# Hybrid conformer and S5 block on 8 cores: the scan's transposes moved from TensorE to DMA, weight casts moved to other stages

## What is computed

```python
h = concat([meta, x])                       # 16 meta tokens + 2048 tokens, width 2048
xn = rmsnorm(h, norm_g)
v_c, g_c, z_c, u_s, z_s, gl_c, gl_s = split(xn @ w_in)      # 5 x 1024 and 2 x 2048 columns
y_c = silu(layernorm(causal_conv31(v_c * sigmoid(g_c)))) * silu(z_c)
y_s = gelu(s5_scan(u_s))                    # 64 groups of 16 channels, 64 complex states each
y_s = y_s * sigmoid(y_s @ w_glu + b_glu) * silu(z_s)
merged = sigmoid(gl_c + b) * (y_c @ w_conv) + sigmoid(gl_s + b) * (y_s @ w_ssm)
out = rmsnorm(h + merged @ w_out, final_g)[meta dropped]
```

## Time and profile before

| | |
|---|---|
| median of 3 runs | 1659.02 us (1658.43 to 1659.34) |
| the profiled execution | 1657.35 us, span of its slowest core 1655.8 us |
| TensorE (PE) busy | 1606.9 us, 97% of the span, mean granted clock 0.99 |
| VectorE (DVE) busy | 746.7 us, 45% |
| ScalarE (ACT) busy | 508.0 us, 31% |
| GpSimd (POOL) busy | 142.5 us, 9% |
| chain that ended last | PE 91%, ACT 3%, DMA 2%, issue 2%, DVE 1% |

### The profile page before, as it was taken

The page is one execution under the profiler, slowest core; times in us unless marked ns, Lnnn a source line. Parts: engine busy times, 40 slices in busy tenths (PEclk is TensorE's granted clock), DMA queues, the critical chain, the costliest instruction groups (busy, mean ns, idle before and its releaser), DMA issues.

```text
span 1655.8 us, 23121 instructions; the slowest of 8 cores (1653.8 to 1655.8 us)
## 1 busy us (share of the span) xinstructions
PE 1606.9 (97%) x8885; PEld 785.3 (47%) x9054; DVE 746.7 (45%) x1126; ACT 508.0 (31%) x741; POOL 142.5 (9%) x228
## 2 busy tenths in 40 slices
PE   5899999999999999999999999999999999999998
PEld 2444555555554444455444444444444444444444
DVE  3673799888840003567625211111111347443333
ACT  4763577777742110003312332111111000021112
POOL 1001333333310000000000000000000000000000
PEclk8999999999999999999999999999999999999999
DMA  9823255999449210024342524022221536455553
GB/s 223 219 87 52 49 118 93 138 136 152 96 92 176 43 19 6 12 36 61 65 57 39 89 52 64 1 38 39 39 38 39 165 115 209 148 172 152 153 153 121
DMA packets 60926, 155.43 MB, mean 94 GB/s; under 512 B 31425, under 2 KB 34625, under 8 KB 51649
## 3 DMA queue, kind: packets, MB, share of 16 engines
q0 software_dynamic: 13456, 58.20, 23.9%
q1 hardware_dynamic: 19906, 88.91, 17.3%
q10 hardware_dynamic: 27456, 6.82, 2.4%
HBM read 178.03 MB, written 40.89 MB: 132 GB/s over the span
## 4 chain that ended last, share of the span: by engine, by line
PE 91%; ACT 3%; DMA 2%; issue 2%; DVE 1%; POOL 0%; ACTq 0%; DVEq 0%; SPq 0%; POOLq 0%
PE ps L257 89%; DMA wu<-wu 2%; PE ps L276 2%; ACT cs L229 1%; DMA xt<-x 1%; ACT L229 1%; DVE xs L245 0%; ACT xs L231 0%; ACT gst L229 0%; ACT tt L229 0%; PE ps L260 0%; ACT jk L231 0%; DVE h L245 0%; DVE pt L235 0%; POOL wu L279 0%
## 5 line engine op out<-in xcount | busy, mean ns | idle before, releaser
L257 PE MATMUL ps<-xm,wr 128*128 128x512 bf16 x1238 | 288.7, 379 | 4.2 <-ACT gst L229 1.9
L257 PE MATMUL ps<-wb,xm 128*128 128x512 bf16 x1000 | 221.6, 381 | 1.7 <-issue 0.6
L257 PE MATMUL ps<-xm,zr 128*128 128x512 bf16 x1000 | 220.6, 379 | 1.3
L257 PE MATMUL ps<-wo,m 128*128 128x512 bf16 (+1 forms) x1019 | 220.1, 376 | 1.1
L257 PEld LDWEIGHTS ps<-xm,wr 128*128 128x128 bf16 x1280 | 119.3, 98 | 128.1 <-issue 5.2
L257 PE MATMUL ps<-xm,gr 128*128 128x512 bf16 x752 | 168.7, 379 | 0.8
L257 PEld LDWEIGHTS ps<-wo,m 128*128 128x128 bf16 x1040 | 101.8, 98 | 119.5
L257 PEld LDWEIGHTS ps<-wb,xm 128*128 128x128 bf16 x1024 | 100.0, 98 | 120.2 <-issue 2.4
L257 PEld LDWEIGHTS ps<-xm,zr 128*128 128x128 bf16 x1024 | 99.9, 98 | 119.2
L231 ACT ACTIVATE jk<-h 128x2048 bf16<-128x2048 f32 (+2 forms) x20 | 31.4, 1569 | 324.3 <-DVE h L245 324.3
L257 PE MATMUL ps<-wu,xm 128*128 128x512 bf16 x496 | 116.4, 389 | 13.9 <-DMA wu<-wu 7.8
(11 more groups left out here) (179 smaller groups left out, 1763.6 us busy)
## 6 DMA issues: line engine op xcount, KB each, us to landing
xt<-x SPq DMA_DIRECT2D x16, 1024.0 KB, 9.1
x<-x SPq DMA_DIRECT2D x16, 1024.0 KB, 8.8
out<-h SPq DMA_DIRECT2D x15, 1024.0 KB, 6.1
wr<-wm POOLq DMA_DIRECT2D x20, 512.0 KB, 11.6
gscr<-gst SPq DMA_DIRECT2D x20, 512.0 KB, 11.8
gr<-gscr SPq DMA_DIRECT2D x20, 512.0 KB, 4.4
wob<-wo POOLq DMA_DIRECT2D x8, 1024.0 KB, 27.7
zr<-wm POOLq DMA_DIRECT2D x16, 512.0 KB, 6.9
```

Source lines behind the costliest of these rows:

```text
L257: return S.op("pe", lambda e: e.matmul(out_, lhsT, rhs, start=start, stop=stop), r, w, signal=signal)
```

## The change

Three things. `ugt(q + 1)` of the loop becomes `ug_dma(q + 1)`: one `dma_start_transpose` on ScalarE's queue, at the end of step 1 and no longer in step 2, and the meta column's copy moves with it; only `ugt(0)` ahead of the loop stays. `btr` becomes one `dma_start_transpose` on ScalarE's queue, at its place. `ug` rows grow from 129 to 144 columns, so that the transposed part starts at a multiple of 32 bytes, and neighbouring tiles are shifted. Third, the casts leave the scan loop: the 20 small ones go to the second half of the gate g projection (8) and to the first v projection (12), the 8 large ones to the first merges, two in each of j = 0 to 3. The diff, without the changed offsets:

```diff
-        UG = [T(f"ug{i}", [128, 4, 2, 129], BF16, UGo[i]) for i in range(2)]
+        UGs = [dsrc() for _ in range(2)]
+        UG = [T(f"ug{i}", [128, 4, 2, 144], BF16, UGo[i]) for i in range(2)]
...
+        def ug_meta(q):
+            s = q % 2
+            uv = UG[s].ap.rearrange("p g r c -> p (g r) c")
+            cp("dve", uv[:, :, 15:16], UGM.ap[:, 4 * q:4 * q + 4, :].rearrange("p g r -> p (g r)").unsqueeze(2),
+               r=(UGMb,), a=(UGb[s],))
...
+        def ug_dma(q):
+            s = q % 2
+            S.op("act", lambda e: e.dma_start_transpose(
+                out=UG[s].ap.rearrange("p g r c -> p (g r) c")[:, :, 16:144],
+                in_=U.ap[:, 4 * q:4 * q + 4].rearrange("p g r t h -> p (g r t h)")),
+                 (UB[q],), (), (UGb[s],), src=UGs[s])
+            ug_meta(q)
...
         def btr(b, par):
             ys = b % 2
-            bk = misc()
-            pT = ps[bk].bitcast(BF16)
-            for t in range(8):
-                tr(pT[:, t * 128:(t + 1) * 128], YST[ys].ap[:, par, t, :], ident, r=(YSTb[ys][par], IDPb),
-                   w=(PB[bk],), signal=(t == 7))
-            cp("dve" if par == 0 else "act", YS.ap[:, b, par * 1024:(par + 1) * 1024], pT, r=(PB[bk],),
-               w=(YSB[b][2 * par], YSB[b][2 * par + 1]))
+            S.op("act", lambda e: e.dma_start_transpose(
+                out=YS.ap[:, b, par * 1024:(par + 1) * 1024].rearrange("p (t c) -> p t c", t=8),
+                in_=YST[ys].ap[:, par].rearrange("p t c -> p (t c)")),
+                 (YSTb[ys][par],), (YSB[b][2 * par], YSB[b][2 * par + 1]), src=YSs[ys][par])
...
-        casts = [("w", 0, i) for i in range(10)] + [("o", n, h) for n in range(4) for h in range(2)]
-        casts += [("w", 1, i) for i in range(10)]
+        casts = [("w", p, i) for p in range(2) for i in range(10)] + [("o", n, h) for n in range(4) for h in range(2)]
...
                     prep_g2(q)
+                    if nx:
+                        ug_dma(q + 1)
                 if st == 2 and nx:
-                    ugt(q + 1)
                     prep_g1(q + 1)
                     prep_g2a(q + 1)
-                if st % 2 == 0:
-                    cast((S.eng["pe"]["src"], S.eng["pe"]["src"].count))
...
                 tok_unit(WB[nb], WBb[nb], j, bk)
+                if nb == 1 and j % 2 == 1:
+                    cast((S.eng["pe"]["src"], S.eng["pe"]["src"].count))
...
             tok_unit(WB[2 + nb], WBb[2 + nb], j, bk)
+            if nb == 0 and j < 12:
+                cast((S.eng["pe"]["src"], S.eng["pe"]["src"].count))
...
                 stt(M0.ap[:, j, n * 512:(n + 1) * 512], MA[2 * tn + 1].ap, 0.5, MA[2 * tn].ap, ALU.mult, ALU.add,
                     r=(MAb[2 * tn], MAb[2 * tn + 1]), w=(M0B[j][n],))
+                if n % 2 == 1:
+                    cast((S.eng["pe"]["src"], S.eng["pe"]["src"].count))
```

More of the change, by code:

```diff
@@ L612, in build @@
         SSb = [t.buf() for t in SS]
-        UGo = (D0 + 90592, D0 + 49344)
-        UG = [T(f"ug{i}", [128, 4, 2, 129], BF16, UGo[i]) for i in range(2)]
+        UGo = (D0 + 90752, D0 + 49344)
+        UGs = [dsrc() for _ in range(2)]
+        UG = [T(f"ug{i}", [128, 4, 2, 144], BF16, UGo[i]) for i in range(2)]
         UGb = [t.buf() for t in UG]
-        CQo = (D0 + 75840, D0 + 51424)
+        CQo = (D0 + 76032, D0 + 51648)
         WT, G1, G2, WV, TT, CM, M7 = [], [], [], [], [], [], []
@@ L627, in build @@
         WTb, G1b, G2b, WVb, TTb, CMb, M7b = [[t.buf() for t in L_] for L_ in (WT, G1, G2, WV, TT, CM, M7)]
-        CSo = (D0 + 82304, D0 + 57312)
+        CSo = (D0 + 82496, D0 + 57536)
         CS = [T(f"cs{i}", [128, 4, 2, NCH], F32, CSo[i]) for i in range(2)]
         CSb = [t.buf() for t in CS]
-        BCT = [T(f"bct{i}", [128, 4, 4, 16], F32, D0 + 92704 + 1024 * i) for i in range(4)]
+        BCT = [T(f"bct{i}", [128, 4, 4, 16], F32, D0 + 93056 + 1024 * i) for i in range(4)]
         BCTb = [t.buf() for t in BCT]
         BCTs = [dsrc() for _ in range(4)]
-        MT = [T(f"mt{i}", [128, 4, 8, 16], F32, D0 + 67648 + 2048 * i) for i in range(4)]
+        MT = [T(f"mt{i}", [128, 4, 8, 16], F32, D0 + 67840 + 2048 * i) for i in range(4)]
         MTb = [t.buf() for t in MT]
-        DM7 = [T(f"dm7{i}", [128, 4, 16], F32, D0 + 81728 + 256 * i) for i in range(2)]
+        DM7 = [T(f"dm7{i}", [128, 4, 16], F32, D0 + 81920 + 256 * i) for i in range(2)]
         DM7b = [t.buf() for t in DM7]
@@ L744, in prep_t @@
                 r=(PB[bk],), w=(TTb[s],))
-        MP = T("mp", [128, 4, 8, 16], F32, D0 + 65600)
+        MP = T("mp", [128, 4, 8, 16], F32, D0 + 65792)
         MPb = [MP.buf(0, 1024), MP.buf(1024, 2048)]
-        MQ = [T("mq0", [128, 2, 8, 16], F32, D0 + 96800), T("mq1", [128, 2, 8, 16], F32, LWOFF + 8224)]
+        MQ = [T("mq0", [128, 2, 8, 16], F32, D0 + 97152), T("mq1", [128, 2, 8, 16], F32, LWOFF + 8224)]
         MQb = [t.buf() for t in MQ]
@@ L795, in ugt @@
             uv = UG[s].ap.rearrange("p g r c -> p (g r) c")
-            cp("dve", uv[:, :, 1:129], pT.rearrange("p (i c) -> p i c", i=8), r=(PB[bk],), a=(UGb[s],))
-            cp("dve", uv[:, :, 0:1], UGM.ap[:, 4 * q:4 * q + 4, :].rearrange("p g r -> p (g r)").unsqueeze(2),
-               r=(UGMb,), a=(UGb[s],))
+            cp("dve", uv[:, :, 16:144], pT.rearrange("p (i c) -> p i c", i=8), r=(PB[bk],), a=(UGb[s],))
+            ug_meta(q)
[5 more added lines that the diff above has]
+                 (UB[q],), (), (UGb[s],), src=UGs[s])
+            ug_meta(q)
         def vmm(g):
             s, gi, v = (g // 4) % 2, g % 4, g % 2
-            rhs = UG[s].ap[:, gi].rearrange("p r c -> p (r c)")
+            rhs = UG[s].ap[:, gi, :, 15:144]
             mm(ps2[v][:, 0:NCH], WV[s].ap[:, gi, 0:128], rhs, True, True, r=(WVb[s], UGb[s]), w=(PB[2 * v],),
@@ L827, in ymm @@
                 o_ = ps[bk][:, g * 128:(g + 1) * 128]
-                mm(o_, UG[s].ap[:, g, par, 1:129], TT[s].ap[:, g].rearrange("p t h -> p (t h)"), True, False,
+                mm(o_, UG[s].ap[:, g, par, 16:144], TT[s].ap[:, g].rearrange("p t h -> p (t h)"), True, False,
                    r=(UGb[s], TTb[s]), w=(PB[bk],))
@@ L837, in ymm @@
                 a=(YSTb[ys][par],))
+        YSs = [[dsrc() for _ in range(2)] for _ in range(2)]
         def btr(b, par):
             ys = b % 2
-            bk = misc()
-            pT = ps[bk].bitcast(BF16)
-            for t in range(8):
-                tr(pT[:, t * 128:(t + 1) * 128], YST[ys].ap[:, par, t, :], ident, r=(YSTb[ys][par], IDPb),
-                   w=(PB[bk],), signal=(t == 7))
-            cp("dve" if par == 0 else "act", YS.ap[:, b, par * 1024:(par + 1) * 1024], pT, r=(PB[bk],),
-               w=(YSB[b][2 * par], YSB[b][2 * par + 1]))
+            S.op("act", lambda e: e.dma_start_transpose(
+                out=YS.ap[:, b, par * 1024:(par + 1) * 1024].rearrange("p (t c) -> p t c", t=8),
+                in_=YST[ys].ap[:, par].rearrange("p t c -> p (t c)")),
+                 (YSTb[ys][par],), (YSB[b][2 * par], YSB[b][2 * par + 1]), src=YSs[ys][par])
         consts()
```

## The result

The changed kernel takes 1681.18 us, median of 4 runs, against 1659.04 before: 1.0136 times as long, 95% interval 1.0122 to 1.015. The forecast was 1649.3 us, faster. (One of the four runs is left out of the ratio, because one die ran at a lower clock in it; the same holds for some runs of the experiments, and full_half has no other, so its time is not used.) The profiled execution took 1680.93 us.

The account below looks back on a forecast made before the run. TensorE was taken to bound the scan loop; 24 of 31 transpose groups at 0.445 us gain 10.7 us, less 1 for long issues, so 1659.0 - 9.7 = 1649.3 us, range 1644 to 1660.5.

Parts of the forecast that it names:

- the shadow in even rounds: Scan loop, even rounds: btr's TensorE groups lie under ScalarE's table run, so 7 groups, 3.1 us, are not gained.
- the 1 us charged for long issues: ScalarE's queue in the scan: 1 us charged in all for transpose issues taking longer, between 0 and 13.8 us.
- some 5: Scan loop: PE's waits for gst grow from 1.9 to some 5 us, in even rounds behind the table run.
- the operations of line 276: Sign of being right: no line 276 operations between 170 and 497 us.
- add up behind the table run: Scan loop, even rounds: both issues, taken as 1.4 us each, fall into ScalarE's busy run from tt to next gst.
- The sum of 2.3 us more per round: ScalarE in the scan: two issues of 1.4 us less half a 1.0 us copy, 2.3 us more per round.
- under 2 us a round: Sign of being right: ScalarE's idle time in the loop falls from 4.8 to under 2 us a round.
- the cover of 6.3 us: Scan loop: ug_dma, issued after g<-mp, has 6.3 us before the first vmm needs ug; landing takes 3.4 us.
- the way free for the transposes: Scan loop: moving the casts gains nothing by itself but keeps the DMA engines free for transposes.
- part 3: Scan loop, landing of transposed data: ug lands inside its cover, btr's output is read only in stage 3; cost nothing.
- Part 2: ScalarE's new work: 31 DMA transposes at 1.4 us, 8 copies fewer; hides thinly in idle time, 1 us charged.
- rival A: Scan loop: longer issues make ScalarE the bound, 1659 to 1695 us; chance 0.05 at its mild end, 0.07 beyond.

Follow-up runs that it names:

- full_half: Changed kernel with the second block 7 transpose of yst only half by DMA, the rest by TensorE; its time is not used, that issue was held 35.80 us.
- casts_only: Kernel before with only the casts moved to their new places: 1657.57 us median.
- casts_back: Changed kernel with block 7 of ys transposed by TensorE and the casts back in the scan loop: 1.0316 times before, 1708.77 us profiled.
- pe7: Changed kernel with block 7 of ys (two transposes behind the scan loop) transposed by TensorE and copied as before: 1648.76 us, 0.9935 of before.
- loads_wait: Changed kernel with the three 2 MB loads behind the loop waiting for block 7's second transpose to complete: 1646.91 us, 0.9918 of before.
- late_tr: Changed kernel with block 7's two transposes issued some 50 us later, in the first half of the gate g projection: 1646.87 us, 0.993 of before.
- one_load: Changed kernel with only the first of three 2 MB loads ahead of block 7's transposes, the others waiting for the second: 1656.51 us, 0.9985 of before.

## Why the prediction was wrong

**The bound and the gain in the loop: right.** Expected were 10.7 us less 1 for all 31 groups. Between the first and the last vmm stand 28 of them, (28 - 7) x 0.445 = 9.3 us, and 9.4 were measured. So the cost of 0.445 us per group and the shadow in even rounds hold (2.9 us of new waits against 3.1), and the 1 us charged for long issues did not show there. PE's waits for gst are 4.8 us where "some 5" were expected. One sign was put wrongly: the operations of line 276 on `u` and `yst` are gone from the loop, but those on `wt`, from `prep_wv`, are still there.

**ScalarE's load in the loop: right in effect, for a partly wrong reason.** The issues are 1.25 us in the median, and none made PE wait beyond the shadow. The fear that they add up behind the table run was too large, because an issue runs beside the operations of ScalarE that stand ahead of it in the text. Here in the changed kernel `btr` stands between the two gst:

```profile
228.68 1.16 ACT L229 ACTIVATE cs<-cs,hpi 128x1032 f32<-128x1032 f32 x1
228.84 1.25 ACTq L857 DMA_TRANSPOSE ys<-yst  x1
229.74 1.25 ACT L229 ACTIVATE gst<-ps,bgh 128x512 bf16<-128x512 f32 x2
```

The issue begins while the Sin runs, before the gst ahead of it has started. The sum of 2.3 us more per round was an overestimate. The busy share can't show it, since it doesn't count DMA issues (76.09 and 75.42 us of 100 before, 75.56 and 78.45 after); but ScalarE's idle time from 180 to 480 us is 79.7 us, 5.0 a round, where "under 2 us a round" was to be seen.

**ug's landing: right in effect, with luck.** It took 3.1 us in the median and 8.8 at most; PE never waited for it in the changed kernel, and 0.3 to 1.2 us in seven others without casts in the loop. But the cover of 6.3 us, counted from the end of g<-mp, was wrong. The issue doesn't wait for its turn among ScalarE's operations:

```profile
219.00 1.25 ACTq L808 DMA_TRANSPOSE ug<-u  x1
219.29 1.15 ACT L229 ACTIVATE cs<-cs,magic 128x1032 f32<-128x1032 f32 x1
220.33 0.86 ACT L229 ACTIVATE wv<-ps 128x512 bf16<-128x512 bf16 x2
221.08 0.73 ACT L229 ACTIVATE g<-mp,nsg 128x512 bf16<-128x512 f32 x1
```

The four operations below it stand ahead of `ug_dma` in the text, yet it goes out first, 2.8 us before g<-mp ends. In the 15 rounds it is 1.4 to 2.8 us early, and the first vmm on its data starts 8.8 to 9.0 us after it. Four of the 15 landings (6.4, 7.1, 8.5 and 8.8 us) were longer than 6.3.

**The casts: right.** They cost nothing where they went, and taking them away gains nothing by itself, as casts_only shows. That they keep "the way free for the transposes" was right too, and is worth 60 us (casts_back).

**The step that failed is in part 3: "btr's output is read only in stage 3: nothing."** It priced the instruction by who waits for its data and left out who stands behind its issue. For the 14 groups in the loop that was harmless. For the last two, which lie outside the loop behind three loads of 2 MB, it cost 32 us (pe7 against the changed kernel: 1681.18 - 1648.76). Part 2 had the ingredient, as it bounded the issue between 1.25 and 3.85 us, and rival A had the mechanism, ScalarE's queue held by issues. But both took the issue's length as a property of the instruction, spread over all rounds, when it depends on what is outstanding on the queue, and can be 35.8 us in one place. Where rival A's 1695 us came from fifteen rounds, the real 1681 came from one event.

The trace of before had two signs of it, unread. The longest ycs issue was the second of a pair, issued at 975.27 us with the first outstanding and weight loads in flight; another pair takes 2.64 us. From the timeline of ScalarE before:

```profile
959.73 2.64 ACTq L1345 DMA_TRANSPOSE ycs<-co  x2
...
973.54 5.58 ACTq L1345 DMA_TRANSPOSE ycs<-co  x2
```

And the DMA issues of before from 478 to 495 us, the very place of `btr(7, .)`, show what anything put there would be stuck behind:

```profile
wb<-wg POOLq DMA_DIRECT2D x1, 2048.0 KB, 18.1
wb<-wv POOLq DMA_DIRECT2D x1, 2048.0 KB, 32.2
wgl<-wglu POOLq DMA_DIRECT2D x1, 2048.0 KB, 45.3
```

The last landed 45.3 us after its issue; in the changed kernel the hold of 35.8 us from 487.05 ends at 522.85, some 2 to 3 us before the load of w_glu issued at 483.29 lands (41.9 us: 525.2), and the first transpose right after it (42.3 us: 525.9). The prediction read the loop's stretches for this and not the 20 us behind it, although two of the 31 edits stand there.

The range (1644.0 to 1660.5) was too narrow for the same reason: the bounds came from rows of other places, and no case had a single blocked instruction in it.

## What to carry to other kernels

A DMA issued from a computing engine's queue has two prices: when its data lands, and how long its issue holds that engine's other work. The second depends on what is outstanding: here it was safe to keep at most one transpose of this size in flight beside bulk loads, and to put the large loads behind the transposes (loads_wait) or the transposes well behind the loads (late_tr). When one edit is made in many places, price each place by its own neighbours, above all the last ones outside the loop. And a large gain in a steady loop can be real, here 9.4 us, while one event at its edge costs three times as much.

## What the runs showed of the hardware

- A DMA transpose's row on ScalarE's queue can be mostly waiting: 1.25 us when free, 35.8 us when held, with the same amount of work. The Trainium skill, "Perfetto Trace Analysis", section on what "DMA-bound" means, says that such a window on the issuing engine is descriptor generation, not data movement. These runs disagree in part: with one load ahead the window is 12.34 us, with three 35.80, so it followed the data movement of other transfers.
- Behind three loads of 2 MB, transposes of 256 KB in all went out on ScalarE's queue in at most 2.5 us each, and with 384 or 512 KB the second was held for over 33 us. Beside casts a second one of 256 KB was taken in two cores (1.43 and 1.50 us) and the third held, so the bytes outstanding are not the whole rule. A pair of 256 KB each without such a backlog goes out in 2.64 us.
- Beside 6 MB of loads issued from POOL, a transpose of 256 KB lands with the last of them: 43.8 us after its issue, where w_glu, issued 4.2 us earlier, took 46.5, and in place of 3.1. Two of 128 KB land as late (44.1 us), while a plain DMA of 512 KB, gscr on SyncE's queue, issued in the same stretch, took 20.7.
- A DMA issue on ScalarE's queue goes out ahead of operations that stand before it in the text (ug's, 1.4 to 2.8 us before g<-mp ended) and overlaps them; what stands behind a held one waits (the gst at 523.01 us starts 0.16 us after the issue's end).
- Behind an idle stretch of 30.05 us TensorE's granted clock was 0.51 (its level of 1.2 GHz), and the 32 matmuls after it took 9.98 us in place of 7.07; behind one of 6.6 us (one_load) it was 0.52, and they took 9.48.

What stays open is which resource limits the outstanding transposes and when it is given back, and whether plain DMAs on the same queue would be held in the same way; neither was tried.
